# Turned activations of six feed-forward halves placed 16 to 128 bytes past a multiple of 1024 bytes, on one Trainium2 core

## The chip, the cores and the metric

One core of one Trainium2 chip runs the whole program in one launch. The metric is the device time of one execution in microseconds (us); the time given for the kernel is the median of its runs.

## The reference

A sequence of 256 tokens of width 1024 in float32 goes through two transformer blocks of one kind (the first with a gated linear attention mixer and a pooling mixer, the second with sparse attention) and one block of another kind (two attention branches with gates). Each block is a feed-forward half, a mixer and a second feed-forward half:

```python
for li in range(DEPTH):                     # DEPTH = 2
    h = h + 0.5 * swiglu(rms_norm(h, ffn1_norm[li]), ffn1_wi[li], ffn1_wo[li])
    h = h + mix(rms_norm(h, mix_norm[li]))  # gla + pool, then dsa
    h = h + 0.5 * swiglu(rms_norm(h, ffn2_norm[li]), ffn2_wi[li], ffn2_wo[li])
h = rms_norm(h, final_norm)
# then the third block, with gate, up and down weights of its own:
x = x + 0.5 * swiglu_2(...);  x = x + mixed @ w_o;  x = x + 0.5 * swiglu_2(...)

def swiglu(x, wi, wo):                      # wi 1024 x 5632, wo 2816 x 1024
    gate, up = jnp.split(x @ wi, 2, axis=-1)
    return (jax.nn.silu(gate) * up) @ wo
```

The six halves are called a1, a2, b1, b2, c1 and c2 in the kernel. Each multiplies 256 x 1024 by two matrices of 1024 x 2816 and then 256 x 2816 by one of 2816 x 1024.

## The kernel before

Every product of weights and activations is made at about float32 precision out of float32r operands: a number is cut into a high part and a low part, and high times high, high times low and low times high are summed in PSUM. Weights come from HBM as pieces of 128 rows x 2048 numbers into `raw` (4 slots), issued by the SP queue in the order of `plan`. ACT copies a piece to `whi` (line 1193, 3 slots), DVE computes `wlo = raw - whi` (line 1632). A slot is taken again when the matmuls of the piece three before are done. Waits are on semaphores whose values are counted in a first pass through the program; the order on each engine is written out by hand.

Activations stand turned (feature on the partition, token along the row). `XS`, the buffer `xt`, holds 8 blocks of 128 features, each with 256 high parts and behind them 256 low parts, 2048 bytes a block. It is one buffer for all normalised inputs, of the halves and of the mixers; PE turns x (line 616), ACT writes the high part with the gain (line 1206), DVE the low part (line 1646). `hT`, the buffers `a1ht_hi`, `a1ht_lo` and so on, holds the 22 blocks of gated activations of a half: ACT writes the high part (line 1257), DVE the low one (line 1723).

Within a half, `wide` makes the gate and up products, a job of 256 output columns at a time, 22 jobs: the weights are the stationary operand (128 x 128) and a whole block of `XS` the moving one. A job is 16 matmuls of line 637 (stationary `whi`, moving 512 columns, that is high and low part) and 16 of line 643 (stationary `wlo`, moving the 256 high parts). The down product is the other way round (`steps`): the stationary operand is a 128 x 128 block of `hT` and the moving one 512 columns of `whi` or `wlo`, three matmuls at a time, lines 563 (high, high), 564 (high activation, low weight) and 565 (low activation, high weight), 264 of them to a half; in c2 the last piece is split otherwise, which leaves 252 of this width there. The mixers' input products use `steps` too, with `XT`, the same buffer as `XS`, as the stationary operand. The moving rows are 512 columns wide in most of them, and 272, 324 and 360 in the first job of each mixer.

Where the buffers lie follows from the order and the sizes in which they are declared, each start rounded up to 32 bytes. In the kernel before, these start at a multiple of 1024 bytes within the partition: `raw`, `whi`, `wlo`, `X`, `xt`, `yt_hi`, `yt_lo`, and `hT`, `GS` and `U` of all six halves. Others do not: `d_q` of the sparse attention, for one, starts 544 bytes past such a multiple.

In a job of width `wd` the moving row of block j starts `4 * wd * j` bytes into the slot:

```python
hi_w, lo_w = (w[0:n, v % SPLIT, j * wd:(j + 1) * wd] for w in (whi, wlo))
h, l = (a[0:n, kt, 128 * tt:128 * tt + 128] for a in (job.act.hi, job.act.lo))
```

Of the kernel before, what the change touches and what calls it, by code (L numbers as in the profile page):

```python
# [22 lines left out]
WARM = 3  # L23
LEVELS = [1, 2, 4, 8, 16, 32, 64]
# [128 lines left out]
class Ffn:  # L153


    def __init__(self, name, x, gate, g0, up, u0, down, XT):
        self.name, self.x = name, x
        self.g = [Job(f"{name}g{i}", gate, [(0, 8, 128)], [(g0 + 256 * i, 256)], XT, ("xt", x)) for i in range(11)]
        self.u = [Job(f"{name}u{i}", up, [(0, 8, 128)], [(u0 + 256 * i, 256)], XT, ("xt", x)) for i in range(11)]
        self.d = [Job(f"{name}d{i}", down, full_blocks(FF), [(512 * i, 512)], None, (name, "ht")) for i in range(2)]  # L160
# [30 lines left out]
def program(nc, T, out):  # L191
    with ExitStack() as ctx:
# [38 lines left out]
        XS = sb("xt", [128, 8, 2, 256], F32R)  # L231
        XT = Turned(XS[:, :, 0, :], XS[:, :, 1, :])
# [10 lines left out]
        whole = sb("whole", [128, 96])  # L243

        def col_jobs(name, w, K, ranges, act, key):
            return [Job(f"{name}{i}", w, full_blocks(K), [r] if isinstance(r, tuple) else r, act, key)
                    for i, r in enumerate(ranges)]
# [10 lines left out]
                                      [[(1536, 16), (0, 256)], (256, 256), (1552, 512), (512, 512), (1024, 512)], XT, ("xt", "a1"))  # L258
# [3 lines left out]
        di, dk, dq0, dq1, dv = col_jobs("dsa", T["odd_w_in"][0], D,  # L262
                                        [(1536, 324), (1024, 256), (0, 512), (512, 512), (1280, 256)], XT, ("xt", "b1"))
        d_out = col_jobs("dsa_out", T["odd_w_out"][0], D, [(0, 512), (512, 512)], YT, ("yt", "dsa"))
        lat, fq, fk, fv, *gate2 = col_jobs("mla", T["w_in_2"][0], D, [[(0, 352), (1888, 8)], (352, 512), (864, 512), (1376, 512)]
                                           + [(1896 + 512 * i, 512) for i in range(4)], XT, ("xt", "c1"))
# [6 lines left out]
        c_out = col_jobs("c_out", T["w_o_2"][0], D, [(0, 512), (512, 512)], XT, ("xt", "mixed"))  # L273
# [260 lines left out]
        def tensor(e):  # L534
# [89 lines left out]
            def ffn(f):  # L624
                name, g, u, d = f.name, f.g, f.u, f.d

                def wide(job, j0=0, j1=8):
# [6 lines left out]
                    def high(j, b):  # L634
                        q.wait_ge(*s_dve[job.key, j])
                        q.wait_ge(*s_hi[v, j])
                        return e.matmul(pair.ap[:, b, :], whi[:, v % SPLIT, 256 * j + 128 * b:256 * j + 128 * b + 128],  # L637
                                        XS[:, j, :, :].rearrange("p h t -> p (h t)"), start=j == 0, stop=j == 7)

                    def low(j, b):  # L640
# [3 lines left out]
                                 XS[:, j, 0, :], start=False, stop=False)  # L644
# [533 lines left out]
        def scalar(e):  # L1178
# [30 lines left out]
            def turn_x(x, n):  # L1209
                q.wait_ge(*s_dve["gains"])  # L1210
                turned(("xt", x, n), XT, 4 * n, lambda i: gains_of[x](4 * n + i))
# [250 lines left out]
            def mla():  # L1462
# [109 lines left out]
                turned(("mixt", 0), XT, 0, None)  # L1572
                unit()
                unit()
                turned(("mixt", 1), XT, 4, None)
# [10 lines left out]
            def x_high(j):  # L1586

                q.wait_ge(*s_gain0["all"])
                q.wait_ge(*s_xt[min(j // 2, 2)]["x"])
                e.mul(XT.hi[:, j, :], XR[:, j, :], gain("f1", j)).then_inc(s_act.mark(("x0", j)), 1)  # L1590
# [19 lines left out]
        def vector(e):  # L1610
# [38 lines left out]
            def turn_x(x, n):  # L1649
                turned(("xt", x, n), ("xt", x), XT, 4 * n, lambda i: gains_of[x](4 * n + i))  # L1650
# [430 lines left out]
            def mla():  # L2081
# [118 lines left out]
                for n in range(2):  # L2200
                    unit()
                    if n:
                        turned(("mixt", 0), ("xt", "mixed"), XT, 0, None)
# [9 lines left out]
                turned(("mixt", 1), ("xt", "mixed"), XT, 4, None)  # L2213
# [8 lines left out]
            def x_low(j):  # L2222

                q.wait_ge(*s_act["x0", j])
                e.scalar_tensor_tensor(XT.lo[:, j, :], XR[:, j, :], gain("f1", j), XT.hi[:, j, :].bitcast(F32),  # L2225
# [187 lines left out]
```

## Time and profile before

| | |
|---|---|
| median of 2 runs | 1460.87 us (1460.78 to 1460.96) |
| span of the profiled execution | 1458.9 us |
| PE busy | 1452.6 us, 7822 matmuls |
| DVE busy | 1002.6 us |
| ACT busy | 778.5 us |
| DMA, HBM read | 264.56 MB, 182 GB/s over the span |

The profiled execution has no time of its own beside its span: the span runs from its first to its last recorded instruction, and the median of the runs is 2.0 us above it. In the rows below a matmul's length overlaps that of the next, because matmuls are pipelined and their ends are modelled. What one of them costs in a stream is the distance from its start to the next one's start. PEld is the loading of stationary operands, DVE is VectorE and ACT is ScalarE.

### The profile page before, as it was taken

Reading aid. Unit: us, or ns where it says so; the run is one execution under the profiler, and the core shown is the slowest. Engines: PE = TensorE matmul, PEld = TensorE weight load, DVE = VectorE, ACT = ScalarE, POOL = GpSimd, SP = SyncE. Lnnn points to the kernel's source line nnn. Section 1 sums busy time; section 2 is a strip of 40 time slices with the busy share of each in tenths; the row PEclk is TensorE's granted clock in tenths of the full one; section 3 lists DMA queues with packets and bytes.
Section 4 is the critical chain, followed back from the end, with each engine's and each line's share of the span. In section 5 each row is a group of like instructions: output and inputs, shape, how many; then the busy total and the mean of one; then the engine's idle time right before and its main releaser. Section 6 shows DMA issues by size and latency. Waiting matters only on the chain.

```text
span 1458.9 us, 18627 instructions
## 1 busy us (share of the span) xinstructions
PE 1452.6 (100%) x7822; PEld 1250.3 (86%) x7822; DVE 1002.6 (69%) x1216; ACT 778.5 (53%) x971; POOL 87.2 (6%) x113
## 2 busy tenths in 40 slices
PE   9999999999999999999999999999999999999999
PEld 7888888888888888888888888888888888888887
DVE  6976466787755867459877664787646987687653
ACT  6654355655534555345665544564435876465542
POOL 0000003000000000006100000000000800000000
PEclk9999999999999999999999999999999999999999
DMA  9855563556556555545455556475556543556552
GB/s 328 277 183 178 160 203 116 168 180 201 179 182 202 187 187 189 186 139 172 150 198 188 189 172 206 154 223 182 187 173 217 188 144 118 173 193 205 178 187 72
DMA packets 205620, 266.82 MB, mean 183 GB/s; under 512 B 6944, under 2 KB 148880, under 8 KB 205280
## 3 DMA queue, kind: packets, MB, share of 16 engines
q1 hardware_dynamic: 204320, 261.23, 54.5%
q0 software_dynamic: 1072, 4.35, 0.8%
q8 instruction: 62, 1.02, 0.3%
q14 instruction: 22, 0.18, 0.0%
q10 hardware_dynamic: 144, 0.05, 0.0%
HBM read 264.56 MB, written 1.05 MB: 182 GB/s over the span
## 4 chain that ended last, share of the span: by engine, by line
PE 96%; DVE 2%; ACT 1%; DMA 0%; issue 0%; DVEq 0%; ACTq 0%
PE ps L637 33%; PE ps L643 17%; PE ps L563 14%; PE ps L565 13%; PE ps L564 13%; PE ps L616 1%; PE ps L717 1%; PE ps L812 1%; DVE wlo L1632 1%; PE ps L750 1%; DVE d_i L2025 0%; DVE d_m L2021 0%; DMA G<-in_gains 0%; DVE d_i L2049 0%; PE ps L751 0%
## 5 line engine op out<-in xcount | busy, mean ns | idle before, releaser
L1632 DVE TENSOR_TENSOR wlo<-raw,whi 128x2048 fp32r<-128x2048 f32 (+5 forms) x275 | 567.4, 2068 | 259.0 <-ACT whi L1193 258.6
L1193 ACT CAST whi<-raw 128x2048 fp32r<-128x2048 f32 (+5 forms) x275 | 474.7, 1732 | 222.8 <-PE ps L565 218.4
L637 PE MATMUL ps<-xt,whi 128*128 128x512 f32 x2112 | 511.2, 391 | 0.5 <-DVE xt L2225 0.5
L637 PEld LDWEIGHTS ps<-xt,whi 128*128 128x128 f32 x2112 | 386.0, 188 | 74.4 <-DVE xt L2225 1.3
L643 PEld LDWEIGHTS ps<-xt,wlo 128*128 128x128 f32 x2112 | 274.0, 191 | 12.3
L643 PE MATMUL ps<-xt,wlo 128*128 128x256 f32 x2112 | 277.7, 283 | 0.0
L563 PE MATMUL ps<-whi,xt 128*128 128x512 f32 (+4 forms) x304 | 112.7, 371 | 0.0
L565 PE MATMUL ps<-whi,xt 128*128 128x512 f32 (+4 forms) x304 | 109.7, 361 | 0.0
L564 PE MATMUL ps<-wlo,xt 128*128 128x512 f32 (+4 forms) x304 | 109.5, 360 | 0.0
L563 PEld LDWEIGHTS ps<-whi,xt 128*128 128x128 f32 x304 | 57.3, 188 | 9.2 <-issue 1.0
L565 PEld LDWEIGHTS ps<-whi,xt 128*128 128x128 f32 x304 | 57.2, 188 | 8.5
L564 PEld LDWEIGHTS ps<-wlo,xt 128*128 128x128 f32 x304 | 57.4, 189 | 7.4
L1206 ACT ACTIVATE xt<-ps,G 128x256 fp32r<-128x256 f32 x64 | 25.1, 474 | 35.6 <-PE ps L616 35.5
L563 PE MATMUL ps<-whi,yt_hi 128*128 128x512 f32 (+3 forms) x108 | 42.7, 395 | 0.0
L565 PE MATMUL ps<-whi,yt_lo 128*128 128x512 f32 (+3 forms) x108 | 41.7, 386 | 0.0
L564 PE MATMUL ps<-wlo,yt_hi 128*128 128x512 f32 (+3 forms) x108 | 41.6, 386 | 0.0
L1222 ACT ACTIVATE junk<-X 128x512 f32<-128x512 f32 x40 | 25.4, 634 | 28.5 <-DVE X L1690 27.3
L1646 DVE SCALAR_TENSOR_TENSOR xt<-ps,G,xt 128x256 fp32r<-128x256 f32 x64 | 26.5, 477 | 15.6 <-ACT xt L1206 15.6
L563 PE MATMUL ps<-whi,a1ht_hi 128*128 128x512 f32 x88 | 34.3, 390 | 0.0
L563 PE MATMUL ps<-whi,a2ht_hi 128*128 128x512 f32 x88 | 34.3, 390 | 0.0
L563 PE MATMUL ps<-whi,b1ht_hi 128*128 128x512 f32 x88 | 34.3, 390 | 0.0
L563 PE MATMUL ps<-whi,b2ht_hi 128*128 128x512 f32 x88 | 34.3, 390 | 0.0
(422 smaller groups left out, 1885.8 us busy)
## 6 DMA issues: line engine op xcount, KB each, us to landing
raw<-in_ffn_wi SPq DMA_DIRECT2D x85, 1024.0 KB, 4.9
raw<-in_ffn_wo SPq DMA_DIRECT2D x40, 1024.0 KB, 5.0
raw<-in_ffn_w_gate SPq DMA_DIRECT2D x22, 1024.0 KB, 5.1
raw<-in_ffn_w_up SPq DMA_DIRECT2D x22, 1024.0 KB, 5.2
raw<-in_ffn_w_down SPq DMA_DIRECT2D x20, 1024.0 KB, 4.9
raw<-in_w_in SPq DMA_DIRECT2D x14, 1024.0 KB, 5.1
raw<-in_even_w_in SPq DMA_DIRECT2D x6, 1024.0 KB, 5.2
raw<-in_ffn_wo SPq DMA_DIRECT2D x8, 512.0 KB, 3.8
```

The costliest lines, as they stand in the source:

```text
L563: e.matmul(o, h, hi_w, start=i == 0 and j == 0, stop=False)
L564: e.matmul(o, h, lo_w, start=False, stop=False)
L565: t = e.matmul(o, l, hi_w, start=False, stop=(end or (v == len(plan) - 2 and tt == 1)) and j == nk - 1)
L616: t = e.transpose(pair.flat[0:n, 256 * b + 128 * tt:256 * b + 128 * tt + 128], halves[tt], ident[:, :])
L637: return e.matmul(pair.ap[:, b, :], whi[:, v % SPLIT, 256 * j + 128 * b:256 * j + 128 * b + 128], XS[:, j, :, :].rearrange("p h t -> p (h ...
L643: e.matmul(pair.ap[:, b, 0:256], wlo[:, v % SPLIT, 256 * j + 128 * b:256 * j + 128 * b + 128], XS[:, j, 0, :], start=False, stop=False)
L717: t = e.matmul(pair.flat[:, w * h:w * h + w], queries(h)[0:n, 128 * tt:128 * tt + 128], keys(h)[0:n, 0:w], start=True, stop=True)
L1193: e.copy(whi[0:n, v % SPLIT, c], raw[0:n, v % RAW, c]).then_inc(s_hi.mark(*[(v, j) for j in js]), 1)
L1206: t = e.mul(act.hi[0:n, kt0 + i, :], pair.flat[0:n, 256 * i:256 * i + 256], 1.0 if gains is None else gains(i)[0:n, :])
L1222: e.activation(junk[:, :], X[:, tt, 512 * n:512 * n + 512], ACT.Square, accum_out=ssq[:, tt, n:n + 1]).then_inc(s_act.mark(("sq", x, n, tt ...
L1632: e.tensor_tensor(wlo[0:n, v % SPLIT, c], raw[0:n, v % RAW, c], whi[0:n, v % SPLIT, c].bitcast(F32), ALU.subtract).then_inc(s_lo.mark(*[(v ...
L1646: t = e.scalar_tensor_tensor(l, src, gains(i)[0:n, :], h.bitcast(F32), ALU.mult, ALU.subtract)
```

## The change

Each normalised input gets a view `XT[x]` of its own into one slightly larger room, `xs_room`, which is declared behind `whole`. The view starts `SHIFT[x]` numbers of 4 bytes into the room; inputs that have no entry start at 0. The two `hT` buffers of a half get 1024 bytes more each and are viewed from an offset that puts them at the same distance past a multiple of 1024 bytes as the half's input. With the sizes declared, `xs_room` itself starts at a multiple of 1024 bytes, and the rooms of `hT` start 128 bytes past one. The distances are 16 bytes for a1 (input "in"), 32 for a2 ("gla"), 64 for b1 ("a2"), 128 for b2 ("dsa"), 80 for c1 ("b2") and 48 for c2 ("mla"). The block `mixed`, stationary in the third block's output product, gets 48. The inputs of the three mixers ("a1", "b1", "c1") stay at 0. Buffers declared behind `xs_room` move by 128 bytes or a multiple of 128; `whi`, `wlo`, `raw` and `X` do not move. No instruction, wait, size or order is changed.

```diff
+SHIFT = {"in": 4, "gla": 8, "a2": 16, "dsa": 32, "b2": 20, "mla": 12, "mixed": 12}
...
-        self.name, self.x = name, x
-        self.g = [Job(f"{name}g{i}", gate, [(0, 8, 128)], [(g0 + 256 * i, 256)], XT, ("xt", x)) for i in range(11)]
+        self.name, self.x, self.XS = name, x, XT[x].XS
+        self.g = [Job(f"{name}g{i}", gate, [(0, 8, 128)], [(g0 + 256 * i, 256)], XT[x], ("xt", x)) for i in range(11)]
...
-        self.hT = Turned(sb(self.name + "ht_hi", [128, 22, 256], F32R), sb(self.name + "ht_lo", [128, 22, 256], F32R))
+        at = (SHIFT[self.x] - 32) % 256
+        h, l = (sb(self.name + part, [128, 22 * 256 + 256], F32R)[:, at:at + 22 * 256].rearrange("p (k t) -> p k t", k=22) for part in ("ht_hi", "ht_lo"))
+        self.hT = Turned(h, l)
...
-        XS = sb("xt", [128, 8, 2, 256], F32R)
-        XT = Turned(XS[:, :, 0, :], XS[:, :, 1, :])
...
+        xs_room = sb("xt", [128, 8 * 512 + 32], F32R)
+
+        def x_turned(x):
+            at = SHIFT.get(x, 0)
+            XS = xs_room[:, at:at + 4096].rearrange("p (k h t) -> p k h t", k=8, h=2)
+            t = Turned(XS[:, :, 0, :], XS[:, :, 1, :])
+            t.XS = XS
+            return t
+
+        XT = {x: x_turned(x) for x in ("in", "a1", "gla", "a2", "b1", "dsa", "b2", "c1", "mixed", "mla")}
...
-                                        XS[:, j, :, :].rearrange("p h t -> p (h t)"), start=j == 0, stop=j == 7)
+                                        f.XS[:, j, :, :].rearrange("p h t -> p (h t)"), start=j == 0, stop=j == 7)
```

The remaining lines of the change replace `XT` by the view of the input concerned, `XT[x]` or `XT["mixed"]`.

## Rows read from the trace of the kernel before

**Rows 1.** The page: span, busy time of three engines, granted clock in 40 slices

```profile
span 1458.9 us, 18627 instructions
...
PE 1452.6 (100%) x7822; PEld 1250.3 (86%) x7822; DVE 1002.6 (69%) x1216; ACT 778.5 (53%) x971; POOL 87.2 (6%) x113
...
PEclk9999999999999999999999999999999999999999
```

**Rows 2.** Groups by line: count, busy us, mean ns, idle before

```profile
L637 PE MATMUL ps<-xt,whi 128*128 128x512 f32 x2112 | 511.2, 391 | 0.5 <-DVE xt L2225 0.5
...
L643 PE MATMUL ps<-xt,wlo 128*128 128x256 f32 x2112 | 277.7, 283 | 0.0
```

**Rows 3.** Waits in total, longest first: us, times, longest us

```profile
ACT whi L1193 <- PE ps L565: 218.4, 76, 4.4
```

**Rows 4.** Windows, two halves' gate and up: PE, PEld, DVE, ACT, POOL busy; clock

```profile
280.20:403.60 123.40, 123.40 (x711) 108.88 (x710) 93.51 (x103) 70.09 (x79) 0.00 (x0) 1.00 0.57 188
...
1271.20:1394.60 123.40, 123.40 (x711) 108.88 (x710) 93.53 (x103) 71.34 (x80) 0.00 (x0) 1.00 0.59 188
```

**Rows 5.** Timeline of PE in half a1; columns: start us, length us

```profile
118.13 3.82 PE L637 MATMUL ps<-xt,whi 128*128 128x512 f32 x16
121.79 2.08 PE L643 MATMUL ps<-xt,wlo 128*128 128x256 f32 x16
123.70 3.59 PE L637 MATMUL ps<-xt,whi 128*128 128x512 f32 x15
```

**Rows 6.** Timeline of PE: half c1's down product, then 360 columns wide

```profile
1100.91 0.39 PE L563 MATMUL ps<-whi,c1ht_hi 128*128 128x512 f32 x1
...
1103.63 0.32 PE L563 MATMUL ps<-whi,xt 128*128 128x360 f32 x1
...
1104.59 0.33 PE L563 MATMUL ps<-whi,xt 128*128 128x360 f32 x1
...
1107.56 1.04 PE L616 MATMUL ps<-ident,X 128*128 128x128 f32 x8
```

**Rows 7.** Timeline of PE: product of 324 columns, each sixth matmul

```profile
650.25 0.31 PE L563 MATMUL ps<-whi,xt 128*128 128x324 f32 x1
...
651.14 0.31 PE L563 MATMUL ps<-whi,xt 128*128 128x324 f32 x1
...
652.02 0.31 PE L563 MATMUL ps<-whi,xt 128*128 128x324 f32 x1
...
652.91 0.31 PE L563 MATMUL ps<-whi,xt 128*128 128x324 f32 x1
...
653.80 1.03 PE L616 MATMUL ps<-ident,X 128*128 128x128 f32 x8
```

**Rows 8.** Timeline of PE: product of 272 columns; twelve matmuls between rows

```profile
190.49 0.28 PE L563 MATMUL ps<-whi,xt 128*128 128x272 f32 x1
...
191.99 0.29 PE L563 MATMUL ps<-whi,xt 128*128 128x272 f32 x1
...
193.50 0.71 PE L616 MATMUL ps<-ident,X 128*128 128x128 f32 x5
```

**Rows 9.** Instructions that touch xt; duration in ns, min/median/max

```profile
L643 PEld LDWEIGHTS ps<-xt,wlo x2112: 187/192/192, 7.5 to 1395.4; 128*128 128x128 f32 x192
...
L1206 ACT ACTIVATE xt<-ps,G x64: 458/475/486, 166.0 to 1279.5; 128x256 fp32r<-128x256 f32 x64
L1646 DVE SCALAR_TENSOR_TENSOR xt<-ps,G,xt x64: 473/476/485, 168.3 to 1280.5; 128x256 fp32r<-128x256 f32 x64
```

**Rows 10.** The same view for a2ht_hi: its loads and its writers

```profile
L563 PEld LDWEIGHTS ps<-whi,a2ht_hi x88: 187/188/190, 404.9 to 465.0; 128*128 128x128 f32 x88
...
L1257 ACT CAST a2ht_hi<-a2U x11: 622/622/625, 312.1 to 407.6; 128x512 fp32r<-128x512 f32 x11
L1723 DVE TENSOR_TENSOR a2ht_lo<-a2U,a2ht_hi x11: 683/684/692, 312.8 to 410.0; 128x512 fp32r<-128x512 f32 x11
```

More of the change, by code:

```diff
@@ L156, in __init__ @@
     def __init__(self, name, x, gate, g0, up, u0, down, XT):
-        self.name, self.x = name, x
-        self.g = [Job(f"{name}g{i}", gate, [(0, 8, 128)], [(g0 + 256 * i, 256)], XT, ("xt", x)) for i in range(11)]
-        self.u = [Job(f"{name}u{i}", up, [(0, 8, 128)], [(u0 + 256 * i, 256)], XT, ("xt", x)) for i in range(11)]
+        self.name, self.x, self.XS = name, x, XT[x].XS
+        self.g = [Job(f"{name}g{i}", gate, [(0, 8, 128)], [(g0 + 256 * i, 256)], XT[x], ("xt", x)) for i in range(11)]
+        self.u = [Job(f"{name}u{i}", up, [(0, 8, 128)], [(u0 + 256 * i, 256)], XT[x], ("xt", x)) for i in range(11)]
         self.d = [Job(f"{name}d{i}", down, full_blocks(FF), [(512 * i, 512)], None, (name, "ht")) for i in range(2)]
@@ L262, in program @@
         di, dk, dq0, dq1, dv = col_jobs("dsa", T["odd_w_in"][0], D,
-                                        [(1536, 324), (1024, 256), (0, 512), (512, 512), (1280, 256)], XT, ("xt", "b1"))
+                                        [(1536, 324), (1024, 256), (0, 512), (512, 512), (1280, 256)], XT["b1"], ("xt", "b1"))
         d_out = col_jobs("dsa_out", T["odd_w_out"][0], D, [(0, 512), (512, 512)], YT, ("yt", "dsa"))
         lat, fq, fk, fv, *gate2 = col_jobs("mla", T["w_in_2"][0], D, [[(0, 352), (1888, 8)], (352, 512), (864, 512), (1376, 512)]
-                                           + [(1896 + 512 * i, 512) for i in range(4)], XT, ("xt", "c1"))
+                                           + [(1896 + 512 * i, 512) for i in range(4)], XT["c1"], ("xt", "c1"))
         qb = [Job(f"qb{i}", T["mla_w_qb_2"][0], [(0, 2, (128, 64))], [c], YT, ("yt", "lat")) for i, c in enumerate([(0, 512), (512, 256)])]
@@ L272, in program @@
             j.k_off = 4
-        c_out = col_jobs("c_out", T["w_o_2"][0], D, [(0, 512), (512, 512)], XT, ("xt", "mixed"))
+        c_out = col_jobs("c_out", T["w_o_2"][0], D, [(0, 512), (512, 512)], XT["mixed"], ("xt", "mixed"))
         def together(a, b):
@@ L643, in low @@
                         e.matmul(pair.ap[:, b, 0:256], wlo[:, v % SPLIT, 256 * j + 128 * b:256 * j + 128 * b + 128],
-                                 XS[:, j, 0, :], start=False, stop=False)
+                                 f.XS[:, j, 0, :], start=False, stop=False)
                     for j in range(j0, min(j1, 7)):
@@ L1210, in turn_x @@
                 q.wait_ge(*s_dve["gains"])
-                turned(("xt", x, n), XT, 4 * n, lambda i: gains_of[x](4 * n + i))
+                turned(("xt", x, n), XT[x], 4 * n, lambda i: gains_of[x](4 * n + i))
             def squares(x, n):
@@ L1571, in mla @@
                 unit()
-                turned(("mixt", 0), XT, 0, None)
+                turned(("mixt", 0), XT["mixed"], 0, None)
                 unit()
                 unit()
-                turned(("mixt", 1), XT, 4, None)
+                turned(("mixt", 1), XT["mixed"], 4, None)
                 unit()
@@ L2202, in mla @@
                     if n:
-                        turned(("mixt", 0), ("xt", "mixed"), XT, 0, None)
+                        turned(("mixt", 0), ("xt", "mixed"), XT["mixed"], 0, None)
                     q.wait_ge(*s_mm[bm[n].name, 1])
@@ L2212, in mla @@
                 unit()
-                turned(("mixt", 1), ("xt", "mixed"), XT, 4, None)
+                turned(("mixt", 1), ("xt", "mixed"), XT["mixed"], 4, None)
                 unit()
```

8 lines of the change are left out of this document (4 added, 4 removed).

## Prediction

> **What bounds the kernel now.** I read the page first. PE is busy for 1452.6 of 1458.9 us, and its granted clock is at the top in all 40 slices, which is the 2.4 GHz level [rows 1]. Then I read the groups by line: the two lines of the gate and up products hold 2112 matmuls each, and the idle time ahead of them is 0.5 us in all [rows 2]. The list of waits shows who is ahead of whom: ACT's weight copies wait 218.4 us for PE [rows 3]. The half's windows say the same from the other side: in 123.40 us of gate and up products PE has no gap, while DVE works 93.5 us and ACT 70 to 71 us [rows 4]. So the makers of weights and activations have some 30 us of room per half. This kernel is a chain of matmuls, each starting a fixed distance behind the last, and the change can cost or bring something only by altering that distance, or by making some other engine over a quarter slower.
>
> The distances come from the timeline. In half a1, sixteen matmuls of 512 columns begin at 118.13 and the narrow ones begin at 121.79: 3.66 us, or 228.8 ns each. Sixteen of 256 columns take from 121.79 to 123.70: 1.91 us, or 119.4 ns each [rows 5]. Both together are 5.57 us a job, 22 jobs are 122.5 us, and the windows of 123.40 us hold these and some turns. In the down product twelve matmuls of 512 columns go from 1100.91 to 1103.63: 226.7 ns each [rows 6]. At 2.4 GHz, a column a cycle, 512 columns are 213.3 ns and 256 are 106.7. Above that stand 13.4 ns on each down matmul, 15.5 on a wide one and 12.7 on a narrow one. This surplus is all that addresses could act on inside PE.
>
> **The change, part by part.** *Instructions, waits, sizes.* None is added or removed, so this part is 0 us. The views only carry other start addresses.
>
> *Moving operand of the gate and up products, 4224 matmuls.* Before, it starts at a multiple of 1024 bytes, and so does every second stationary block beside it (the others lie 512 bytes further). After, it starts 16 to 128 bytes past one. The trace of before has no line 637 at another address, but it has moving operands there: the first job of each mixer, whose block j starts 4 x width x j bytes into the slot. For 324 columns the four starts are 0, 1296, 2592 and 3888 bytes, that is 0, 16, 32 and 48 past a multiple of 64. The six matmuls at each start take 0.89, 0.88, 0.89 and 0.89 us [rows 7]: 148 ns each wherever they start, the one at 16 bytes no slower than the one at 0. For 272 columns the starts are 0, 64, 128 and 192 past a multiple of 1024. The first two blocks take 1.50 us and the last two 1.51, 125 and 126 ns each [rows 8]. For 360 columns the starts are 0, 416, 832 and 224 past such a multiple, and here the first six take 0.96 us and the 18 later ones 2.97 [rows 6]: 160 ns against 165. So three widths give 0, 0 and 5 ns for leaving the multiple of 1024. I take 0, by the 324 and 272 rows, because they hold the distances of the change, 16, 32 and 48 past a multiple of 64 and 64 and 128 past one of 1024, whereas the 360 rows have 224 to 832. The ends are +5 ns and, by the second start of the 324 rows, 0.01 us over six matmuls or -1.7 ns.
>
> *Stationary operand of the down products, 1572 matmuls of 512 columns.* `hT` now starts 16 to 128 bytes past the multiple and the moving weights stay. No row shows a shifted stationary float32r block. Its load has a length of 188 ns in the trace [rows 10]. That isn't what it costs in a stream: in the narrow run a load of the same form, 192 ns long, is done for every matmul, one each 119.4 ns [rows 5, 9]. A down matmul allows 226.7. A shifted load would have to take 107 ns more before it were late, so I cost it at 0, covered by the matmul in flight. As the relative place of the two operands is all that could matter besides, I give it the same upper end of +5 ns.
>
> *Writers.* ACT and DVE write `xt` in 475 and 476 ns a block [rows 9], and `hT` in 622 and 684 ns for each of 11 chunks in a half [rows 10]. If every one of these took twice as long, a half would have 11 x 0.68 + 8 x 0.48 = 11.4 us more on DVE and 10.6 on ACT, under the 30 us of room [rows 4]. The turn of x at the start of a half lies nearer to the path: PE waited 0.5 us there in all [rows 2], and doubling that is +0.5 us. I take 0. If the cover were gone, the next thing late would be `wlo`, and PE would stand at line 643.
>
> *Buffers behind `xs_room`.* They move by multiples of 128 bytes. `GS` and `U` go from 0 to 128 past a multiple of 1024, the mixers' buffers from one odd place to another (`d_q` stood at 544). Only ACT, DVE and the small float32 matmuls use them, and the room above covers the first two. 0 us.
>
> The sum is 1460.9 + 0 = 1460.9 us. The profiled span is 1458.9 and the runs' median lies 2.0 above it; the sum changes neither. Upper end of the unknown costs: (2112 + 1572) x 5 ns = 18.4 us, and 0.5 from the writers and 1 us of play around it, 1481 us. The narrow matmuls add nothing to that, since the 5 ns apply to the moving stream, and I hold that the load and not the stream sets their distance: 119.4 ns for 256 columns against 125 for 272, where a cost by columns would have them 6.7 apart too, so this is a choice and not shown. Lower end: 3684 x 1.7 ns = 6.3 us, 1454.6 us; with the same play 1453.
>
> Here a rule of the Trainium skill can be weighed. The rows show a surplus of 13.4 ns on a warm matmul of 512 columns [rows 6]. "TensorE: Matmul & The Clock Gate", Back-to-back issue gap, gives an isolated gap of N / 2.4 + 2.5 ns, 215.8 ns at 512. The trace doesn't agree: it has 226.7. By that rule, if the shared multiple of 1024 were what holds this kernel above it, the sum would be 3684 x 10.9 ns = 40 us less, an estimate of 1421 us. The same page (Step-by-step: what each phase is for) says that the load of the stationary operand and the moving stream have read ports of their own, which would leave addresses nothing to undo; no row here can show a port.
>
> **Rivals.** *1. The surplus is a collision of two streams that start at the same place, and the shift removes it: faster.* For it speaks that every wide matmul of before has both operands at multiples of 512 bytes and that a surplus is there at all, the same in each half. Against it speak the 324 and 272 rows: their moving blocks leave that place by the very distances of the change, and the surplus stays, 148 - 135.0 = 13 ns and 125.4 - 113.3 = 12 ns [rows 7, 8]. If it holds, 13.4 ns go from 1572 down matmuls and from 2112 wide ones: 49 us, 1412 us; with only half of the surplus 1436. Chance 0.07. The rule on the gap above is this rival's, and its 1421 lies between the two.
>
> *2. A stream that doesn't start on 64 bytes pays its surplus twice: slower.* The place is lines 637 and 643 of the four halves at 16, 32, 80 and 48 bytes. It decides as soon as the second surplus isn't hidden behind the load. The price is 352 x (13.4 + 12.7) ns = 9.2 us a half, 36.7 for four: 1498 us; were all six hit, 55 us and 1516. For it speaks only that lines 637 and 643 themselves have never been off their place in this trace; against it, the 324 rows at 16 and 48 bytes. Chance 0.13, more than the rows alone would give, because PE has no gap that could absorb a single ns.
>
> *3. A small cost as in the 360 rows.* 5 ns on the wide matmuls alone is 10.6 us, 1471; with the down ones 1479. It is slower, within what counts as the same. Chance 0.15.
>
> *4. The change doesn't do what it says.* The distances hold only if `xs_room` begins at a multiple of 1024, which follows from the declared sizes. If it didn't, all would be displaced by one constant, and the cases above would apply as they are; it has no price of its own and is part of the forecast.
>
> **How the numbers follow.** No change by more than a few us, 1454 to 1467: 0.65. Rival 3: 0.15. Rival 2: 0.13. Rival 1: 0.07. What a measurement of this kernel can tell from no change is taken as 2%, 29 us. Rival 1 is then faster (0.07), as its smaller version stays about at the line, rival 2 slower (0.13), the rest 0.80. The forecast is that of the likeliest, 1461. The range goes from 1453 to 1481: it takes in the forecast, rival 3 and both ends of the unknown costs, and leaves rivals 1 and 2 out, 0.20 together.
>
> **What the profile after would show.** The gate and up part of each half again 123.4 us, with one distance of 228.8 and 119.4 ns in all six, says that the address doesn't matter. A half that differs from the others names its distance: since each has another, the six windows are six readings. Rival 1 would show runs of 16 wide matmuls well under 3.6 us; rival 2, over 3.8 us in a1, a2, c1 and c2 and not in b1 and b2; rival 3, 3.74. The down products should keep 226.7 ns; if they change and the wide ones don't, it is the stationary operand. The three mixers' input products, whose operands don't move, should stay to the 0.01 us and are the control. Wrong would make it above all a rule by which the chip treats a moving block of 2048 bytes otherwise than one of 1296, since the 512-column form is the one that I have at a single address only; or writers that slow down by more than two, which would show as PE idle ahead of line 643.

## Result and the profile after

The changed kernel takes 1472.93 us (median of 2 runs, 1472.83 to 1473.03) against 1460.87: ratio 1.0083, 95% interval 1.0064 to 1.0102. That is 12.1 us slower, inside the range that was given (1453 to 1481) but not the forecast itself, which was no change. The page of its profile begins so, to be read beside [rows 1]:

```profile
span 1470.9 us, 18627 instructions
...
PE 1464.7 (100%) x7822; PEld 1246.8 (85%) x7822; DVE 1002.6 (68%) x1216; ACT 777.8 (53%) x971; POOL 87.2 (6%) x113
...
PEclk9999999999999999999999999999999999999999
```

PE is busy for 12.1 us more; DVE has the same 1002.6 us, ACT 0.7 less, the clock is the same and the count of instructions is the same. So PE neither waits nor does more. Its matmuls start further apart. The list of waits says it from the other side, as ACT now waits longer for PE (218.4 us before [rows 3]):

```profile
ACT whi L1204 <- PE ps L576: 227.2, 76, 4.6
```

(Lines of the kernel after are 11 higher on PE and ACT: the wide matmul is L648, the narrow one L654, the down product L574 to L576.) The writers and the loads of `a2ht_hi`, beside [rows 10], in nanoseconds least, median, most:

```profile
L574 PEld LDWEIGHTS ps<-whi,a2ht_hi x88: 187/188/190, 406.3 to 468.1; 128*128 128x128 f32 x88
...
L1268 ACT CAST a2ht_hi<-a2U x11: 616/619/624, 313.0 to 409.1; 128x512 fp32r<-128x512 f32 x11
```

Neither moved. The timeline of PE in half a2 (inputs at 32 bytes), a whole job from wide run to wide run, beside [rows 5]:

```profile
372.50 3.89 PE L648 MATMUL ps<-xt,whi 128*128 128x512 f32 x16
376.24 2.03 PE L654 MATMUL ps<-xt,wlo 128*128 128x256 f32 x16
378.10 3.89 PE L648 MATMUL ps<-xt,whi 128*128 128x512 f32 x16
```

Sixteen wide matmuls now take 3.74 us instead of 3.66, and sixteen narrow ones 1.86 instead of 1.91: the first kind lost 5 ns each and the second gained 3. In half b1 (64 bytes) it goes otherwise:

```profile
552.60 3.82 PE L648 MATMUL ps<-xt,whi 128*128 128x512 f32 x16
556.25 2.05 PE L654 MATMUL ps<-xt,wlo 128*128 128x256 f32 x16
558.14 3.84 PE L648 MATMUL ps<-xt,whi 128*128 128x512 f32 x16
561.82 1.98 PE L654 MATMUL ps<-xt,wlo 128*128 128x256 f32 x16
563.63 3.82 PE L648 MATMUL ps<-xt,whi 128*128 128x512 f32 x16
```

Two jobs take 11.03 us where before they took 11.14 (twice 5.57): this half is faster than before. Its narrow runs alternate between 1.89 and 1.81 us, at the same addresses. In the down product of a2, twelve matmuls apart, beside the 2.72 us of [rows 6]:

```profile
429.67 0.40 PE L574 MATMUL ps<-whi,a2ht_hi 128*128 128x512 f32 x1
...
432.47 0.40 PE L574 MATMUL ps<-whi,a2ht_hi 128*128 128x512 f32 x1
```

2.80 us or 233.3 ns each, 6.6 ns more, although it was only the stationary operand that moved. The table adds all of it up from the timelines. Gate and up is the time from the first wide matmul of a half to its last; down is the sum over all 264 distances of a half, each from the start of a matmul to the start of the next one on PE (258 in c2, whose narrower ones are left out); in us, before and after.

| half | distance, bytes | gate and up | down product |
|---|---|---|---|
| a1 | 16 | 122.76, 123.23 | 59.96, 60.92 |
| a2 | 32 | 123.41, 124.08 | 59.96, 61.69 |
| b1 | 64 | 123.41, 122.42 | 59.96, 61.68 |
| b2 | 128 | 123.41, 124.57 | 59.96, 61.43 |
| c1 | 80 | 123.41, 124.22 | 59.96, 61.32 |
| c2 | 48 | 123.41, 124.48 | 58.49, 60.20 |
| sum of differences | | +3.2 | +9.0 |

12.2 us of a span that grew by 12.0. The mixers and the rest, 360.8 us before and 360.7 after (the span without the columns above), stayed in all, and the mixers' input products did to 0.1 us each. One product in there did not: the third block's output product, whose stationary block `mixed` now stands 48 bytes past the multiple. Its 96 matmuls of 512 columns take 0.6 us more, 6.3 ns each, and other distances gave as much back. Three quarters of the loss lie in the down products.

### The profile page after: what moved, and what is told of

Its sections match the earlier page's. It is cut to its first block, busy times and chain, and to the rows that moved or that the text cites. A ratio compares the mean times of both kernels' runs of the same rounds, so it can differ in the third digit from the quotient of the medians.

```text
span 1470.9 us, 18627 instructions
## 1 busy us (share of the span) xinstructions
PE 1464.7 (100%) x7822; PEld 1246.8 (85%) x7822; DVE 1002.6 (68%) x1216; ACT 777.8 (53%) x971; POOL 87.2 (6%) x113
## 4 chain that ended last, share of the span: by engine, by line
PE 96%; DVE 2%; ACT 1%; DMA 0%; issue 0%; SPq 0%; DVEq 0%; ACTq 0%
PE ps L648 33%; PE ps L654 17%; PE ps L574 14%; PE ps L576 14%; PE ps L575 14%; PE ps L627 1%; PE ps L728 1%; PE ps L823 1%; DVE wlo L1643 1%; PE ps L761 1%; DVE d_i L2036 0%; DVE d_m L2032 0%; DMA X<-in_x_turned 0%; DVE d_i L2060 0%; PE ps L762 0%
## 5 line engine op out<-in xcount | busy, mean ns | idle before, releaser
L648 PE MATMUL ps<-xt,whi 128*128 128x512 f32 x2112 | 517.8, 394 | 0.5 <-ACT whi L1204 0.3
L648 PEld LDWEIGHTS ps<-xt,whi 128*128 128x128 f32 x2112 | 385.2, 188 | 80.1 <-DVE xt L2236 1.5
L654 PEld LDWEIGHTS ps<-xt,wlo 128*128 128x128 f32 x2112 | 270.2, 188 | 13.7
L654 PE MATMUL ps<-xt,wlo 128*128 128x256 f32 x2112 | 273.7, 280 | 0.0
L574 PE MATMUL ps<-whi,xt 128*128 128x512 f32 (+4 forms) x304 | 112.8, 371 | 0.0
L576 PE MATMUL ps<-whi,xt 128*128 128x512 f32 (+4 forms) x304 | 109.8, 361 | 0.0
L574 PEld LDWEIGHTS ps<-whi,xt 128*128 128x128 f32 x304 | 57.3, 188 | 9.3 <-issue 1.0
L576 PEld LDWEIGHTS ps<-whi,xt 128*128 128x128 f32 x304 | 57.3, 188 | 8.6
L574 PE MATMUL ps<-whi,yt_hi 128*128 128x512 f32 (+3 forms) x108 | 42.7, 396 | 0.0
L576 PE MATMUL ps<-whi,yt_lo 128*128 128x512 f32 (+3 forms) x108 | 41.7, 386 | 0.0
L574 PE MATMUL ps<-whi,a2ht_hi 128*128 128x512 f32 x88 | 34.9, 396 | 0.0
L574 PE MATMUL ps<-whi,b1ht_hi 128*128 128x512 f32 x88 | 34.8, 396 | 0.0
L576 PE MATMUL ps<-whi,a2ht_lo 128*128 128x512 f32 x88 | 34.8, 396 | 0.0
L575 PE MATMUL ps<-wlo,a2ht_hi 128*128 128x512 f32 x88 | 34.8, 396 | 0.0
```

What stands on the lines that cost most here:

```text
L574: e.matmul(o, h, hi_w, start=i == 0 and j == 0, stop=False)
L575: e.matmul(o, h, lo_w, start=False, stop=False)
L576: t = e.matmul(o, l, hi_w, start=False, stop=(end or (v == len(plan) - 2 and tt == 1)) and j == nk - 1)
L654: e.matmul(pair.ap[:, b, 0:256], wlo[:, v % SPLIT, 256 * j + 128 * b:256 * j + 128 * b + 128], f.XS[:, j, 0, :], start=False, stop=False)
```

## Experiments

Runs were made beside the kernel before, which took 1460.8 to 1460.9 us each time. A "job" below is 16 wide and 16 narrow matmuls, and its figures are means over the last 18 jobs of a half, from the start of a matmul to the start of the next one on PE. Where distances are given to the ns, they are read from the starts of single matmuls in the trace.

**wide_only and down_only: which operand.** The first puts `hT` back at a multiple of 1024, the second the inputs.

```diff
-        at = (SHIFT[self.x] - 32) % 256      # wide_only, in Ffn.room
+        at = -32 % 256
...
-            at = SHIFT.get(x, 0)             # down_only, in x_turned
+            at = 0
```

> Only the turned inputs are shifted (16, 32, 64, 128, 80 and 48 bytes); the gated activations stand at a multiple of 1024 bytes again. In the changed kernel the six gate and up parts took 3.2 us more than before and the six down products 9.1 us more. Theory A, that each matmul's distance follows from where its own two operands start, expects the down products back at 226.7 ns and the gate and up parts as in the changed kernel: 1464.1 us. Rival B, that ACT and DVE take the time by writing to shifted places, expects no such split: the whole moves with the number of shifted writes, 1467 or so, and the down products between 227 and 233 ns.

> Only the gated activations, stationary in the down product, are shifted; the inputs stand at a multiple of 1024 bytes. Theory A expects 233 ns a matmul in all six down products and the gate and up parts as before the change, 123.4 us each: 1460.9 + 9.1 = 1470.0 us, so that three quarters of the loss come from the operand whose load seemed covered. If the load's own length were what matters (the rival by which a shifted load is slow), the loads of these blocks show more than 188 ns.

wide_only took 1464.1 us (1463.75 to 1464.28; ratio 1.0022, interval 1.0013 to 1.0032), down_only 1470.19 us (ratio 1.0064, 1.0048 to 1.0081). The excesses, 3.3 and 9.3 us, make 12.6 together and the whole change 12.1. In wide_only the timeline of the same down product as above, and then in down_only:

```profile
429.77 0.39 PE L574 MATMUL ps<-whi,a2ht_hi 128*128 128x512 f32 x1
...
432.49 0.39 PE L574 MATMUL ps<-whi,a2ht_hi 128*128 128x512 f32 x1
```

```profile
429.74 0.40 PE L574 MATMUL ps<-whi,a2ht_hi 128*128 128x512 f32 x1
...
432.54 0.40 PE L574 MATMUL ps<-whi,a2ht_hi 128*128 128x512 f32 x1
```

226.7 and 233.3 ns. And the loads of the shifted blocks in down_only, least, median, most:

```profile
L574 PEld LDWEIGHTS ps<-whi,a2ht_hi x88: 187/188/190, 406.4 to 468.2; 128*128 128x128 f32 x88
```

Their recorded length didn't change, so a load that became long is not what the trace shows. The two parts are separate and nearly add up, as theory A had it. That wide_only met its 1464.1 us to the digit is in part luck: the gate and up parts took 2.6 us more there and not 3.2, and `mixed`, which that run leaves at 48 bytes, made the other 0.6. The inputs of down_only stand at a multiple of 1024 bytes again, but some 23 KB further into the partition than before; their wide matmuls take 228.7 ns against 228.8, so it isn't the larger move that costs.

One down product shows that the distance in bytes isn't all. In a1, with 16 bytes in both kernels, it took 60.9 us in the changed kernel and 61.7 in down_only. The timeline of the changed kernel, twelve matmuls apart, first ahead of the eight matmuls that turn x (they start at 164.61) and then behind them:

```profile
161.11 0.40 PE L574 MATMUL ps<-whi,a1ht_hi 128*128 128x512 f32 x1
...
163.91 0.40 PE L574 MATMUL ps<-whi,a1ht_hi 128*128 128x512 f32 x1
```

```profile
170.25 0.39 PE L574 MATMUL ps<-whi,a1ht_hi 128*128 128x512 f32 x1
...
172.97 0.39 PE L574 MATMUL ps<-whi,a1ht_hi 128*128 128x512 f32 x1
```

2.80 us and then 2.72: from 233.3 ns the stream fell to 226.7, the time of undisplaced blocks, and stayed there to the end of the product, with no address changed. few_writes below does the same, down_only and the other halves of the changed kernel don't; in sweep_3 a1's product, at 60 bytes, goes from 233.3 to 230.0 ns in the same place. So a displaced block need not cost, and the stream's past has a say.

**all_64: absolute or relative.** 64 bytes more are declared ahead of everything that matters.

```diff
+        pad = sb("pad", [128, 16])
         raw = sb("raw", [128, RAW, 2048])
```

> The kernel before with 64 bytes more declared ahead of the weight buffers: raw, weights, inputs and gated activations all stand 64 bytes past a multiple of 1024, and their places relative to each other are as before. Theory A, in the form that only the relative place counts, expects 1460.9 us, 226.7 and 120 ns. Rival C, that an operand must itself stand at a multiple of 1024 bytes, expects some 233 ns on every matmul of 512 columns: 3684 x 6.5 ns = 24 us more, or at least 12 us as in the changed kernel.

1460.69 us (ratio 0.9999, interval 0.999 to 1.0009), and the timeline is that of before:

```profile
371.19 3.82 PE L638 MATMUL ps<-xt,whi 128*128 128x512 f32 x16
374.85 2.08 PE L644 MATMUL ps<-xt,wlo 128*128 128x256 f32 x16
376.76 3.82 PE L638 MATMUL ps<-xt,whi 128*128 128x512 f32 x16
```

Rival C falls. No operand has to stand at a multiple of 1024 bytes; what counts is where activations stand relative to the weights.

**few_writes: is it the other engines?**

```diff
+                c = c if v < SPLIT else slice(c.start, c.start + 16)   # in high, ACT, and in low, DVE
```

> The changed kernel, but from the fourth piece of weights on ACT and DVE write only 16 of its columns per copy, so the weights of later pieces are mostly those of the first three; DMA, matmuls and all places are those of the changed kernel. Theory A expects the same distances to the ns in all six halves (231.5, 233.2, 229.0, 233.0, 231.0 and 233.2 ns for wide matmuls, 232 to 234 in the down products). Rival B expects the distances to fall towards 226.7, as 900 us of ACT and DVE work on the weight buffers are gone.

DVE's busy time fell from 1002.6 to 485.9 us and ACT's from 777.8 to 376.4. The time was 1471.0 us in one run, and a job in half a2 is what it was in the changed kernel (3.74 and 1.86 us there, 3.73 and 1.87 here):

```profile
372.61 3.89 PE L648 MATMUL ps<-xt,whi 128*128 128x512 f32 x16
376.34 2.03 PE L654 MATMUL ps<-xt,wlo 128*128 128x256 f32 x16
378.21 3.89 PE L648 MATMUL ps<-xt,whi 128*128 128x512 f32 x16
```

The means over the half agree to 0.1 ns in all six halves. With half of ACT's and DVE's work gone nothing of the pattern went. The copies left out wrote to `whi` and `wlo`, which don't stand shifted; what excludes the writing to shifted places is the two runs above. In wide_only nothing shifted is written during the jobs measured, and their wide distances are those of the changed kernel to 0.1 ns; and the changed kernel's a2 writes its shifted blocks until 411 us, while its down product takes 233 ns a matmul until 469. So rival B falls. Of the 1.9 us that the run is under the changed kernel, 1.7 lie outside the halves (359.0 us of rest against 360.7).

**sweep_1, sweep_2 and sweep_3: thirty-six distances.** Two tables in place of one, so that inputs and gated activations of a half have distances of their own (sweep_1 shown; `xs_room` has room for 512 bytes).

```diff
+SHIFT = {"in": 24, "gla": 28, "a2": 48, "dsa": 64, "b2": 80, "mla": 96}
+DOWN = {"in": 1, "gla": 2, "a2": 6, "dsa": 24, "b2": 48, "mla": 64}
...
+        at = (DOWN[self.x] - 128) % 256
```

> Twelve more distances in one kernel. Inputs of a1, a2, b1, b2, c1, c2 stand 96, 112, 192, 256, 320 and 384 bytes past a multiple of 1024; their gated activations 4, 8, 24, 96, 192 and 256 bytes. Two forms of theory A: by lines of 64 bytes, 192, 256, 320 and 384 all read like 64 bytes in the changed kernel (229.0 and 115.8 ns) and 96 like 32 (233.2 and 116.8); by another period (512 bytes, say) the readings differ from each other and none of these repeats a known one. In the down products any distance but 0 costs: 232 to 234 ns for all six, 4 bytes included. A rival, that only whole lines of 16 bytes matter, expects 226.7 for 4 and 8 bytes.

> Twelve further distances: inputs at 160, 224, 448, 512, 72 and 56 bytes, gated activations at 512, 384, 320, 160, 448 and 960 bytes. If the period of the effect is 512 bytes, the input at 512 reads as at 0 (226.8 and 119.5 ns) and the gated activations at 512 take 226.7 ns; if it is 1024, both read like the others. 56 and 72 bytes read like 64 if there is a broad best place near it, and like 32 to 48 (233 ns) if 64 is a point. No distance of the gated activations is expected under 226.7 ns.

> Distances read modulo 256 bytes, which is the period that the first two sweeps showed. Inputs of a1, a2, b1, b2, c1, c2 at 4, 68, 108, 116, 188 and 208 bytes; gated activations at 60, 124, 188, 196, 208 and 240. If places of 64 bytes are points, 68, 60, 124, 188 and 196 read like the rest (232 ns and more); if the good places 0, 64, 112 and 192 are broad, the ones beside them are within 1 ns of them. An input at 4 bytes tells whether the wide matmul, like the down one, loses its 226.8 ns by a single element. No job is expected under the 5522 ns of the 64-byte distance.

They took 1467.99, 1473.05 and 1481.72 us, one run each. An input at 256 bytes in sweep_1 gives the job of before, 3.66 and 1.91 us:

```profile
823.63 3.82 PE L649 MATMUL ps<-xt,whi 128*128 128x512 f32 x16
827.29 2.08 PE L655 MATMUL ps<-xt,wlo 128*128 128x256 f32 x16
829.20 3.14 PE L649 MATMUL ps<-xt,whi 128*128 128x512 f32 x13
```

At 192 bytes the wide run loses (3.72) and the narrow one gains (1.82):

```profile
553.85 3.89 PE L649 MATMUL ps<-xt,whi 128*128 128x512 f32 x16
557.57 1.98 PE L655 MATMUL ps<-xt,wlo 128*128 128x256 f32 x16
559.39 2.96 PE L649 MATMUL ps<-xt,whi 128*128 128x512 f32 x12
```

At 116 bytes, in sweep_3, both lose (3.84 and 1.94), the worst found:

```profile
804.59 4.00 PE L649 MATMUL ps<-xt,whi 128*128 128x512 f32 x16
808.43 2.11 PE L655 MATMUL ps<-xt,wlo 128*128 128x256 f32 x16
810.37 4.00 PE L649 MATMUL ps<-xt,whi 128*128 128x512 f32 x16
```

All readings with an input's distance, ns per wide matmul, per narrow one and per job, with those of the kernels before and after:

| bytes | wide | narrow | job | | bytes | wide | narrow | job |
|---|---|---|---|---|---|---|---|---|
| 0, 256, 512 | 228.8 | 119.5 | 5574 | | 96 | 233.6 | 120.0 | 5658 |
| 4 | 237.6 | 122.2 | 5758 | | 108 | 229.9 | 119.2 | 5586 |
| 16 | 231.9 | 116.7 | 5577 | | 112 | 231.1 | 116.2 | 5556 |
| 32 | 233.5 | 116.8 | 5605 | | 116 | 240.0 | 121.4 | 5784 |
| 48 | 233.3 | 118.2 | 5624 | | 128, 384 | 233.0 | 118.7 | 5627 |
| 56 | 232.2 | 119.9 | 5633 | | 160 | 234.5 | 118.5 | 5649 |
| 64, 320 | 229.6 | 115.5 | 5522 | | 188 | 230.3 | 120.0 | 5605 |
| 68 | 237.4 | 118.4 | 5694 | | 192, 448 | 233.3 | 113.7 | 5551 |
| 72 | 234.0 | 120.8 | 5677 | | 208 | 230.3 | 119.2 | 5592 |
| 80 | 231.4 | 119.2 | 5610 | | 224 | 233.3 | 118.6 | 5631 |

(At 64 bytes b1 of the changed kernel has 115.8 and 5526; the other readings there are those of the table.)

And a down product by the distance of the gated activations, time of the half over its count of distances: 227.1 ns at 0, 256 (c2: 226.7) and 512; 228.4 at 240; 229 at 192, 448 and 960 (that is 192 by 256); 230.8 to 231.0 at 8, 24 and, in the changed kernel, 16; 232 to 234 at 4, 32, 48, 60, 64, 80, 124, 128, 160, 188, 196, 208, 320 and 384; 234.5 at 96. Each is one half of one run with one input beside it, and a1 above took 230.8 or 233.6 at the same 16 bytes, so differences of 3 ns among them prove little.

What follows: the gate and up pattern repeats every 256 bytes, at every distance that was read twice (256 and 512 as 0, 320 as 64, 384 as 128, 448 as 192). The good places that were tried from above are sharp: 4 bytes further than 0, 64 or 112 cost 8 to 9 ns on each wide matmul. From below it is otherwise: 4 bytes short of 112 or 192 the wide matmul is even 1 and 3 ns cheaper (229.9 against 231.1, 230.3 against 233.3), and the narrow one is 3 and 6 ns dearer. So the rival with lines of 16 bytes falls, and so does the form of theory A with a period of 64. The down product is best at 0 and never below it. The wide run is best at 0 too, but the narrow one isn't: 113.7 ns at 192, 115.5 at 64.

**x64_all: all inputs at 64 bytes, gated activations at 0.**

```diff
+SHIFT = {"in": 16, "gla": 16, "a2": 16, "dsa": 16, "b2": 16, "mla": 16}
+DOWN = {"in": 0, "gla": 0, "a2": 0, "dsa": 0, "b2": 0, "mla": 0}
```

> The inputs of all six halves stand 64 bytes past a multiple of 1024, the gated activations at one. Half b1 of wide_only has this form: its gate and up part took 122.36 us against 123.39 before. Theory A expects that for all six, 6 x 1.03 = 6.2 us less than before, 1454.7 us, a version faster than both kernels. A rival, that b1 is fast for another reason than its 64 bytes (its place in the program), expects no gain in the other halves: 1460 us.

1454.45 us (1454.26 to 1455.19, 5 runs), ratio 0.9958, interval 0.9944 to 0.9971: 6.3 us faster than the kernel before and 18.5 than the changed one. The gate and up parts took 122.36 us in five halves and 121.90 in a1. The rival falls: place in the program plays no part. Again the narrow runs take 1.88 (118 ns) and 1.81 us (113 ns) by turns:

```profile
552.47 3.84 PE L649 MATMUL ps<-xt,whi 128*128 128x512 f32 x16
556.15 1.98 PE L655 MATMUL ps<-xt,wlo 128*128 128x256 f32 x16
557.96 3.82 PE L649 MATMUL ps<-xt,whi 128*128 128x512 f32 x16
561.62 2.05 PE L655 MATMUL ps<-xt,wlo 128*128 128x256 f32 x16
563.51 3.84 PE L649 MATMUL ps<-xt,whi 128*128 128x512 f32 x16
```

**wlo_64: own operands or the neighbours'.** `wlo` is declared behind `xs_room`, 64 bytes past a multiple of 1024; all else stands at one.

```diff
-        wlo = sb("wlo", [128, SPLIT, 2048], F32R)
...
+        xs_room = sb("xt", [128, 8 * 512 + 16], F32R)
+        wlo = sb("wlo", [128, SPLIT, 2048], F32R)
+        behind = sb("behind", [128, 16])
```

> Only wlo stands 64 bytes past a multiple of 1024; whi, inputs and gated activations are at one. Theory A, each matmul by its own two operands: the wide matmuls (whi with xt) keep 226.8 ns, the narrow ones (wlo with xt) fall from 119.5 to 116 or less, and of the three kinds in the down product only the ones with wlo as the moving operand rise to 233. If it is the neighbour in the queue that counts (a load is made while the matmul before it runs), the kinds next to it in the down product rise instead or as well, and the wide ones stay, as their neighbours are of whi.

1468.39 us, one run. In the gate and up part the wide run kept its 3.66 us, and the narrow one fell to 1.88 (117.5 ns):

```profile
551.81 3.82 PE L650 MATMUL ps<-xt,whi 128*128 128x512 f32 x16
555.47 2.05 PE L656 MATMUL ps<-xt,wlo 128*128 128x256 f32 x16
557.35 3.82 PE L650 MATMUL ps<-xt,whi 128*128 128x512 f32 x16
```

In the down product, twelve matmuls:

```profile
430.22 0.39 PE L576 MATMUL ps<-whi,a2ht_hi 128*128 128x512 f32 x1
...
433.00 0.40 PE L576 MATMUL ps<-whi,a2ht_hi 128*128 128x512 f32 x1
```

231.7 ns, and not on one kind of three: the means of the half a2 are 232.3 (high with high), 232.0 (low weights moving) and 232.4 (low activation), all 5 to 6 ns up, though only the middle kind has an operand that moved. So the first form of theory A, each matmul by its own two operands, is wrong where kinds are mixed. A displaced operand is paid for by its neighbours in the stream too: three matmuls together take 15.4 ns more, where a stationary block 64 bytes off costs 6.6 ns and one 192 bytes off 2.2.

The expectation also overlooked a sign. Here the stationary operand of a narrow matmul lies 64 bytes further than the moving one, in x64_all the moving one than the stationary one; modulo 256 this is the distance of 192 bytes, where the table has 113.7 ns. The narrow matmuls took 117.9, so neither reading of the distance gives the time of this mixture.

**both_64: distance 0 for the wide, 64 for the narrow.** The high weights of gate and up pieces stand 64 bytes further, as the inputs do; those of other pieces stay.

```diff
+        def whi(v):
+            job = plan[v][0]
+            at = 2112 * (v % SPLIT) + (16 if len(job.blocks) == 1 and job.blocks[0][1] == 8 else 0)
+            return whi_room[:, at:at + 2048]
```

> Inputs of the halves and the high weights of their gate and up pieces stand 64 bytes past a multiple of 256, the low weights and everything in the down products at one. So wide matmuls have distance 0 and narrow ones 64. If the pair of a matmul's own operands decides, wide matmuls keep 226.8 ns and narrow ones have the 115.6 ns of x64_all: a job of 5574 - 16 x 4.0 = 5510 ns, 12 ns less than x64_all, and with the dearer turns at the run's ends between 5485 and 5520; 132 jobs make 1449.5 to 1454 us. If the neighbour decides, as the down products of wlo_64 suggest, narrow matmuls stay at 117.9 as in wlo_64 (5546 ns a job) and the time is 1457 us.

1460.85 us (1460.71 to 1461.21), ratio 1.0, interval 0.9991 to 1.0009. The narrow run has 117.8 ns in every job and never 113.4, and the wide run costs more than in wlo_64, 3.69 against 3.66 us:

```profile
550.43 3.85 PE L653 MATMUL ps<-xt,whi 128*128 128x512 f32 x16
554.12 2.05 PE L659 MATMUL ps<-xt,wlo 128*128 128x256 f32 x16
556.00 3.85 PE L653 MATMUL ps<-xt,whi 128*128 128x512 f32 x16
```

The job is 5577 ns. Neither expectation holds: narrow matmuls are as the second had it, and the wide ones are dearer than both had them. The first ten wide ones after a switch are uneven, 241, 238, 233, 236, 224, 231, 236, 228, 232 and 231 ns; only from the eleventh on do they take 226.7, the time of their own pair. Before the change five were uneven. So pairing the best wide distance with a good narrow one gains nothing here: what a matmul takes depends on what ran before it.

**splits: does the order inside a job pick the fast narrow run?**

```diff
+AHEAD = {"a1": (14, 14), "a2": (14, 13), "b1": (14, 12), "b2": (14, 11), "c1": (14, 10), "c2": (13, 14)}
...
+                        for j, b in order[:k]:      # k = AHEAD[name][job in u]
+                            high(j, b)
+                        for j, b in order:
+                            low(j, b)
```

> x64_all with another order inside a job: so many of the 16 wide matmuls stand ahead of the 16 narrow ones, in gate and up jobs: 14 and 14 in a1 (as before), 14 and 13 in a2, 14 and 12 in b1, 14 and 11 in b2, 14 and 10 in c1, 13 and 14 in c2. All addresses are those of x64_all. There narrow matmuls of the same addresses took 117.8 ns in one job and 113.4 in the next, by turns. If the address pair alone set the distance, this could not change: half of the narrow runs at 113.4 in all six halves. If the rhythm in which the run of wide matmuls ends decides, the share of runs at 113.4 differs between the halves, from none (a job of 5560 ns) to all (5485 ns).

1454.76 us in one run. In a2, with 15 and 17 wide matmuls between the narrow runs:

```profile
363.77 3.61 PE L650 MATMUL ps<-xt,whi 128*128 128x512 f32 x15
367.22 1.98 PE L656 MATMUL ps<-xt,wlo 128*128 128x256 f32 x16
369.03 4.05 PE L650 MATMUL ps<-xt,whi 128*128 128x512 f32 x17
372.92 2.05 PE L656 MATMUL ps<-xt,wlo 128*128 128x256 f32 x16
374.81 3.61 PE L650 MATMUL ps<-xt,whi 128*128 128x512 f32 x15
```

1.81 and 1.89 us by turns, as before. Of the last 18 narrow runs, 9, 10, 7, 9, 7 and 8 took 113 ns a matmul in a1 to c2, and a job took 5522, 5518, 5531, 5522, 5531 and 5527 ns. In b1 and in c1 five runs at 118 ns follow one another before the turns begin. So the spread from none to all that the rhythm was expected to give did not come.

The rhythm itself isn't refuted by that, and the starts of the single matmuls speak for it. At this distance the wide matmuls aren't evenly spaced; they go 226, 229, 232 ns over and over. Of the 304 full narrow runs over inputs 64 bytes off (all of x64_all and splits, b1 of the changed kernel, of wide_only and of few_writes, and c1 of sweep_1, at 320), the 140 at 113 ns all follow a wide run that ends on the step of 232 ns, and the 164 at 118 all follow one that ends on 226 or 229; there is no exception. It explains the turns, too. Behind a fast narrow run the wide one begins with 226, and its sixteenth step is 226 again, so the next narrow run is slow. Behind a slow one it begins with 233 and 236, then 229, and its sixteenth step is 232. An order inside a job only shifts where the runs end, and after a few jobs they fall back into turns. So at the same addresses the place in this three-step pattern goes with the time of the run that follows. What in the engine keeps the pattern, and whether it sets the narrow run's time or shares a cause with it, isn't shown.

## Why the prediction was right or wrong

*What bounds the kernel.* Right. PE is busy for all but 6 us in both kernels, and the 12.0 us of the span are wider distances between its matmuls, 12.2 us of them in the six halves.

*Stationary operand of the down products, costed at 0.* This is the step that failed, and it carries 9.0 of the 12 us. The reasoning was that a load of 188 ns, done elsewhere every 119.4 ns, leaves 107 ns of cover under a matmul of 226.7. The load did stay as long as it was, and the cover was there; the distance grew all the same, to 233 ns. A cover in time says nothing about whether two operations disturb each other while they overlap. The bound that I attached because relative place might matter besides, 5 ns on 1572 matmuls or 7.9 us, pointed at the right thing and was still too low: it came to 5.7 ns (9.0 us over 1572). The 96 matmuls of the third block's output product, also with a displaced stationary block, had no term at all; they cost 0.6 us.

*Moving operand of the gate and up products, costed at 0.* Wrong by 3.2 us, and by more in each kind than in the sum. I took the 324 and 272 rows over the 360 rows, since they held the distances of the change. The sums over those rows are right: six matmuls that start at 0 take as long as the ones at 16, 32 and 48 bytes. But they didn't carry over to 512 columns, where the same 16, 32 and 48 bytes cost 3 to 5 ns. The rows held a warning. The six 360-column matmuls whose operands stand together take 160 ns one like the other, and the later ones 158 to 169; the six 324-column ones at 0 already go from 143 to 151, so they were no undisturbed case to measure a disturbance by. Wide matmuls at the five other distances lost 2.6 to 4.7 ns each on average. The narrow ones gained 0.3 to 3.7 ns, for which the prediction had no term at all: it held their 119.4 ns for the time of a load, and at 192 bytes they take 113.7.

*Writers, buffers behind, instructions, clock.* Right, 0 us as far as the runs show; ACT and DVE have the same lengths, the clock is at the top in all 40 slices again, and taking half of the two engines' work away changed no distance in the halves. (The sum of doubled writers on DVE makes 11.3 us and not 11.4, which changes nothing.)

*Rival 1, a collision that the shift removes.* The direction exists, at 64 bytes (half b1: 1.0 us less) and for narrow matmuls alone; its price of 49 us doesn't. No down product took less than before (227.1 ns a matmul, 226.7 in c2).

*Rival 2, a stream not on 64 bytes pays twice.* Wrong by kind: 16, 32 and 48 bytes cost a wide matmul 3 to 5 ns and not 13, and 128, a multiple of 64, costs as much as they do.

*Rival 3, a small cost as in the 360 rows.* This is what happened, at 0.15. Its 5 ns on wide and down matmuls made 1479; the measured 1472.9 lies between that and the forecast, because the wide matmuls lost 3.3 ns on the mean of the six halves and not 5, and the narrow ones gave about 4 us back (their gains of 2.8, 2.7, 3.7, 0.8, 0.3 and 1.3 ns in a1 to c2, times 352 each). The range held because it had taken in this rival and the unknown term of the stationary operand, and partly by luck: the 5 ns a matmul in it were too few for the down products, and wide matmuls that lost less and narrow ones that gained made up for it. The forecast itself was 0, the sum of two terms that both came out otherwise.

*The sign in the profile after* had been named rightly: six halves, six readings, the mixers as the control. The larger part of the loss stood where it expected 226.7 ns, in the down products; its rule for that case, that it would then be the stationary operand, is what down_only showed.

*Two rules weighed.* The Trainium skill, "TensorE: Matmul & The Clock Gate", Step-by-step: what each phase is for, says that stationary load and moving stream have read ports of their own and that loading does not take read bandwidth from the running matmul. The runs don't show ports, but they show that for these float32r operands the two addresses are not independent: down_only moved stationary blocks alone and each down product took 5 to 7 ns more per matmul. By the other rule, which the same page of the Trainium skill states under Back-to-back issue gap, an isolated gap of N / 2.4 + 2.5 ns, a matmul of 512 columns would take 215.8 ns; in steady runs the best of all distances tried took 226.7.

*Still open.* What inside PE or its memory repeats every 256 bytes was not found, nor what carries the three-step pattern that goes with narrow runs of 113 and 118 ns, or why a1's down product fell from 233.3 to 226.7 ns in mid-product. That it is not ACT's or DVE's writing, and not the absolute address, is shown (for a common shift of 64 bytes and for inputs moved by 23 KB). A collision between the load of one matmul's stationary block and the moving stream of the one before was only argued; alone it doesn't fit wlo_64, where one load in three would meet a displaced stream and all three kinds of matmul took 5 to 6 ns more.

## What to carry to other kernels

In a stream of float32r matmuls without gaps, the place of the activations relative to the weights, modulo 256 bytes, was worth up to 4% of the matmul time here (5784 ns a job at 116 bytes against 5574 at 0), and 4 bytes sufficed for 3% (5758). Keep both at the same place, and if the stream has narrow matmuls, try 64 bytes between them by measurement: the time at one distance also depended on what ran before. When a buffer is grown, moved or declared elsewhere, look at the distance from start to start of the matmuls before looking for any other reason. And where an overlap is costed at nothing, ask not only if the cover is long enough but also if the two share something; if the trace has no row of them at the new place, the bound belongs into the sum, not only into the range.

## What was not expected of the hardware

- The period of 256 bytes: jobs at 256 and 512 bytes took 5574 ns as at 0, at 320 5522 as at 64, at 384 5627 as at 128 and at 448 5551 as at 192.
- A single float of displacement: 237.6 ns per wide matmul at 4 bytes against 228.8 at 0, and 240.0 at 116 bytes against 231.1 at 112.
- The common place is best for 512 moving columns (226.7 ns in a steady run) and not for 256 (119.5 ns, against 113.7 at 192 bytes).
- Two narrow runs with the same addresses take 113.4 and 117.8 ns per matmul by turns, in every job pair of x64_all, and all 304 looked at are told apart by the step (226, 229 or 232 ns) on which the wide run before them ends.
- A down product with its stationary blocks 16 bytes off fell from 233.3 to 226.7 ns a matmul in mid-stream, behind eight matmuls of another kind.
- Moving `wlo` alone slowed matmuls that don't read it: 232.3 ns for high with high in the down product, against 227.5 before.
